# Every second chunk of expert weights asked for from ScalarE's queue

## The reference

```python
def hierarchical_moe(h, router_group, router_expert, w_gate, w_up, w_down):
    ...
    y = jnp.zeros_like(h)
    for e in range(N_EXPERTS):
        hid = jax.nn.silu(h @ w_gate[e]) * (h @ w_up[e])
        y = y + combine[..., e:e + 1] * (hid @ w_down[e])
    return y
```

## Time and profile before

| | |
|---|---|
| median of 3 runs | 3169.62 us (3167.96 to 3172.79) |
| profiled execution, its time | 3166.09 us |
| its span, from first to last instruction | 3164.3 us |
| granted TensorE clock, mean | 0.977 |
| PE busy | 2975.3 us (94%) |
| DVE, ACT busy | 1923.8 us, 1635.7 us |
| chunks asked for by SP in the whole kernel | 568, of which 192 in the expert stage |
| expert stage | the chunks are asked for from 843 to 1520 us of the span |

### The profile page before, as it was taken

One profiled execution on the slowest core, in us unless ns is written; L12 is line 12 of the kernel. 1 busy time (PEld: TensorE's weight loads), 2 busy tenths in 40 slices (PEclk: granted clock), 3 DMA queues, 4 the chain that ended last, 5 costly groups with the idle time before them and its releaser, 6 DMA issues.

```text
span 3164.3 us, 41302 instructions
## 1 busy us (share of the span) xinstructions
PE 2975.3 (94%) x16783; PEld 2592.6 (82%) x16783; DVE 1923.8 (61%) x2200; ACT 1635.7 (52%) x1942; POOL 175.2 (6%) x111
## 2 busy tenths in 40 slices
PE   4799999998979999999699999999989999999998
PEld 3798998897867777777599998888869999888886
DVE  3558644533468787888556675555545758555554
ACT  3354444433457777767555644444445554445443
POOL 0403100000000000000000100000000110000000
PEclk8899999999989999999899999999989999999999
DMA  4454557543649898989554555555545545555553
GB/s 150 142 165 147 204 189 243 201 149 120 201 154 352 286 345 284 336 291 360 180 167 160 173 187 186 173 176 183 180 138 190 172 149 194 179 185 173 174 186 133
DMA packets 322887, 629.31 MB, mean 199 GB/s; under 512 B 18425, under 2 KB 28178, under 8 KB 321298
## 3 DMA queue, kind: packets, MB, share of 16 engines
q1 hardware_dynamic: 319776, 617.03, 57.5%
q10 hardware_dynamic: 2642, 8.67, 0.7%
q0 software_dynamic: 288, 1.05, 0.1%
HBM read 619.36 MB, written 7.34 MB: 198 GB/s over the span
## 4 chain that ended last, share of the span: by engine, by line
PE 72%; DVE 10%; ACT 7%; issue 5%; DMA 5%; ACTq 0%; POOL 0%; DVEq 0%; SPq 0%; POOLq 0%
PE pairs L597 14%; PE pairs L599 14%; PE pairs L598 14%; PE pairs L607 8%; PE pairs L609 7%; PE pairs L611 7%; DVE w_lo L1739 5%; ACT w_hi L1240 2%; DMA raw<-in_w_gate_dram 2%; PE misc L985 2%; DMA raw<-in_w_up_dram 2%; PE misc L883 1%; PE misc L720 1%; PE misc L927 1%; ACT scratch L1574 1%
## 5 line engine op out<-in xcount | busy, mean ns | idle before, releaser
L1739 DVE TENSOR_TENSOR w_lo<-raw,w_hi 128x1024 fp32r<-128x1024 f32 x1136 | 1405.7, 1259 | 937.8 <-ACT w_hi L1240 930.8
L1240 ACT ACTIVATE w_hi<-raw 128x1024 fp32r<-128x1024 f32 x1136 | 1178.1, 1058 | 979.6 <-PE pairs L599 581.4
L597 PE MATMUL pairs<-w_hi,a_hi 128*128 128x512 f32 x1664 | 663.5, 399 | 27.5 <-DVE w_lo L1739 22.8
L599 PE MATMUL pairs<-w_hi,a_lo 128*128 128x512 f32 x1664 | 651.6, 392 | 0.0
L598 PE MATMUL pairs<-w_lo,a_hi 128*128 128x512 f32 x1664 | 651.6, 392 | 0.0
L607 PE MATMUL pairs<-a_hi,w_hi 128*128 128x256 f32 x1920 | 557.4, 290 | 47.6 <-DVE w_lo L1739 47.6
L609 PE MATMUL pairs<-a_lo,w_hi 128*128 128x256 f32 x1920 | 549.0, 286 | 0.0
L611 PE MATMUL pairs<-a_hi,w_lo 128*128 128x256 f32 x1920 | 548.5, 286 | 0.0
L607 PEld LDWEIGHTS pairs<-a_hi,w_hi 128*128 128x128 f32 x1920 | 373.8, 195 | 55.1 <-issue 31.4
L597 PEld LDWEIGHTS pairs<-w_hi,a_hi 128*128 128x128 f32 x1664 | 314.4, 189 | 111.8 <-DVE w_lo L1739 33.6
L609 PEld LDWEIGHTS pairs<-a_lo,w_hi 128*128 128x128 f32 x1920 | 374.3, 195 | 0.4
(11 more groups left out here) (312 smaller groups left out, 2315.5 us busy)
## 6 DMA issues: line engine op xcount, KB each, us to landing
raw<-in_w_in_dram SPq DMA_DIRECT2D x232, 1024.0 KB, 5.1
raw<-in_w_out_dram SPq DMA_DIRECT2D x80, 1024.0 KB, 5.0
raw<-in_w_gate_dram SPq DMA_DIRECT2D x64, 1024.0 KB, 7.2
raw<-in_w_up_dram SPq DMA_DIRECT2D x64, 1024.0 KB, 7.3
raw<-in_w_down_dram SPq DMA_DIRECT2D x64, 1024.0 KB, 6.1
raw<-in_xattn_wk_dram SPq DMA_DIRECT2D x16, 1024.0 KB, 5.0
raw<-in_xattn_wv_dram SPq DMA_DIRECT2D x16, 1024.0 KB, 5.0
raw<-in_xattn_wq_dram SPq DMA_DIRECT2D x16, 1024.0 KB, 5.1
```

Of the source, the lines that this page charges most:

```text
L597: nc.tensor.matmul(o, hi[:, k, tok], w_hi[:, s, q, :], start=k == 0, stop=False)
L599: m = nc.tensor.matmul(o, lo[:, k, tok], w_hi[:, s, q, :], start=False, stop=last)
L1240: a.activation(w_hi[:, i % HSLOTS], raw[:, i // 2, 2 * (i % 2):2 * (i % 2) + 2, :], ACT.Copy).then_inc(hi_done, 1)
L1739: v.tensor_tensor(w_lo[:, i % HSLOTS], raw[:, i // 2, 2 * (i % 2):2 * (i % 2) + 2, :], w_hi[:, i % HSLOTS].bitcast(F32), ALU.subtract).the ...
```

## The change

In the expert stage chunks 0 and 2 of every unit stay with SP. Chunks 1 and 3 are asked for by ACT, on its own queue, apart from those of the first unit. ACT has the request for chunk 1 of the next unit behind its half 5, and that for chunk 3 of the same unit behind its half 1. Each request waits for the same two counts as before. There are 47 x 2 = 94 such requests. The other stages are unchanged.

```diff
@@ SyncE @@
-            for g in range(GROUPS):
-                for i in range(PER_GROUP):
-                    e = PER_GROUP * g + i
-                    for r, ww in enumerate((w_gate, w_up)):
-                        for c in range(CHUNKS):
-                            chunk(c, moe_h(g, 2 * i + r) + 2 * c + 2, ww[:, e, 4 * c:4 * c + 4, :])
-                for n in range(4):
-                    for c in range(CHUNKS):
-                        chunk(c, moe_h(g, E0 + n) + 2 * c + 2,
-                              w_down[:, PER_GROUP * g + c, :, n * COLS:(n + 1) * COLS])
+            for n in range(GROUPS * UNITS_G):
+                for c in range(CHUNKS):
+                    if n == 0 or c % 2 == 0:
+                        chunk(c, H["moe"] + n * HALVES + 2 * c + 2, moe_chunk(n, c))
@@ ScalarE, in run() @@
                     state[0] += 1
+                    n = (h - H["moe"]) // HALVES
+                    if h % HALVES == 5 and 0 <= n < GROUPS * UNITS_G - 1:
+                        load(n + 1, 1)
+                    if h % HALVES == 1 and 0 < n < GROUPS * UNITS_G:
+                        load(n, 3)
+
+            def load(n, c):
+
+                count = H["moe"] + n * HALVES + 2 * c + 2
+                act.wait_ge(hi_done, count)
+                act.wait_ge(lo_done, count)
+                act.dma_start(raw[:, c], moe_chunk(n, c)).then_inc(landed[c], 16)
```

More of the change, by code:

```diff
@@ L459, in moe_h, with moe_chunk @@
             return H["moe"] + HALVES * (UNITS_G * g + i)
+        def moe_chunk(n, c):
+            g, i = n // UNITS_G, n % UNITS_G
+            if i < E0:
+                return (w_gate, w_up)[i % 2][:, PER_GROUP * g + i // 2, 4 * c:4 * c + 4, :]
+            return w_down[:, PER_GROUP * g + c, :, (i - E0) * COLS:(i - E0 + 1) * COLS]
         def gather_bank(g, c):
```

## The result

The changed kernel takes 3173.32 us (median; 3169.15 to 3178.63), the kernel before on the same chip 3166.30 us (3160.65 to 3172.79). The ratio is 1.0022, with the interval 1.0015 to 1.0029: the change costs 7.0 us. The profiled execution of the changed kernel took 3170.03 us, 3.9 us more than that of before, so the traces show only a good half of the loss, and single traces scatter by as much. The times decide here, the traces show where to look.

What follows compares the result with a forecast made beforehand. PE was taken as the bound, busy 2975.3 of 3164.3 us, with 23.9 us idle in the expert stage. The terms 0 + 0 + 5 + 0 = +5 us on the median 3169.62 gave 3174.6 us; whole range 3156 to 3197 us.

Steps and rivals of the forecast that it cites:

- What SP gives up: Expert stage: SP's 0.37 us issue is hidden within 3.00 us per chunk, so taking 94 requests off it frees 0 us.
- What ACT pays: Gate units after half 5: ACT's request makes `hidden_hi` 0.30 us late once per expert, 16 x 0.30 = 4.8, say 5 us.
- When ACT asks: Expert stage: ACT's requests come at the same time or at most about 1.4 us later, within the slack; cost 0.
- the slack of 2.6 us: Full stretch: a request may be about 2.6 us later before the DMA engines run dry.
- What two queues do to one another: Full stretch: older chunks land later, but engines stay full and landings stay 3.00 us apart; 0, bounds 0 and 21 us.
- the prediction's own signs of being right: Last gate and up units of a group: DMA share 1.00 with 350 GB/s, stretch within 47.98 + 4 x 0.5 us.
- rival A: Full stretch: shared engines delay the older chunk, 21 us on top of the 5, 3195.6 us; chance 0.30.
- A's two signs: Expert stage: landing times of SP's chunks above 7.8 us, and ACT's waits for landings above 63.5 us in total.
- Rival B: Full stretches: two queues keep the DMA engines better filled, above 360 GB/s, 12 us faster, 3157.6 us; chance 0.20.
- The doubt held against B: Full stretch: the engines' share is 1.00 already, start-of-kernel transfers have partly longer rows, and PE has little idle time.
- Rival C: Gate units: the 0.30 us falls into waits that are there anyhow, nothing reaches PE; 3169.6 us, chance 0.20.

Runs made afterwards that it cites:

- e7: Against the changed kernel: from the second unit on ACT asks for all four chunks on its one queue, 188 requests; 3167.64 us, ratio to before 1.0007.
- e2: Against the changed kernel: SP asks for all chunks; ACT keeps its 94 waits and issues, each moving only 8 numbers; 3168.67 us, ratio to before 1.0012.
- e4: Against the changed kernel: the 16 requests directly ahead of `hidden_hi` go back to SP, ACT keeps 78; 3172.39 us, ratio to before 1.0023.
- e8: Against the changed kernel: SP asks for all chunks, chunk 1 only once ACT signals behind half 6; 3171.01 us, ratio to before 1.0018.
- e1: Against the changed kernel: ACT asks for chunk 1 behind half 6 instead of half 5; 3188.92 us, ratio to before 1.0079.
- e11: Against the kernel before: SP asks for 512 KB halves, each when its half slot is free, and ACT waits per half; 3150.80 us, ratio 0.9956.
- e3: Against the changed kernel: GpSimd instead of ACT asks for chunks 1 and 3 on its own queue; 3182.10 us, ratio to before 1.0054.

## Why the prediction was right, and where it was not

The forecast was 3174.6 us, +5 us, which is less than the 6.3 us that the prediction took as the least a measurement can tell from no change; measured were +7.0 us. The sign and the size hold. That 3174.6 lies only 1.3 us from the measured 3173.32 is luck: the median it started from, of three executions, was 3.3 us above that of twenty, and the step was 2 us too small. The account behind the step holds in part.

- **What SP gives up: 0.** Nothing in the runs speaks against it: from the second unit on e7 takes all requests off SP and isn't faster. The Trainium skill, page "DMA: Bandwidth & Descriptors", section "Issuing engines are not separate DMA queues", was right that a second issuing engine brings no bandwidth here. That it costs some is what these runs add.
- **What ACT pays: 16 x 0.30 us.** The mechanism is in the trace as described: request to next instruction 0.42 us (0.41 forecast), DVE short of half 6, PE's `w_lo` later. The size was about 12 x 0.33 = 4 us, not 16 x 0.30: the first of the four units with `hidden_hi` in a group has 6.30 us with and without the request. One of the four is a down unit, where the prediction put the cost at 0; it goes from 5.67 to 6.00 us like the gate units. On one queue this is about what is lost (e7 2.2 us, e2 3.8 us). With two queues no gain is seen when it is taken away (e4, 1.0023 against 1.0022).
- **When ACT asks: 0.** ACT's requests start on the median 0.09 us after the slot is free, SP's 0.07, as forecast; between 940 and 1525 us the latest begins 0.48 us after it. But the slack of 2.6 us isn't free even on one queue: e8, with one chunk in four late by 0.90 us on average, costs 5.7 us. On two queues the same lateness costs 25 us (e1).
- **What two queues do to one another: 0.** This is the step that failed, "landings still come 3.00 us apart". Landings became irregular: 7.8 and 9.5 us on the median for the chunks of one matrix by queue, single chunks up to 10.3 us (10.7 in e4) where the longest took 9.3 us, single waits of 2.7 us (3.6 us in e4) where the longest was 2.3 us, the share down to 0.95 and 51.07 us in one stretch, where the prediction's own signs of being right were 1.00 and no more than 49.98 us. By the timed runs the second queue costs 7.3 us without the request ahead of `hidden_hi` (e4 against the kernel before) and 3 to 5 us on top of ACT's price (the change against e2 and e7). That is rival A's mechanism at a sixth to a third of its 21 us, which assumed half the slack lost once per expert. Of A's two signs one came in part: single chunks of SP's took 10.3 us, but SP's medians rose to no more than 7.8 us in the stretch, and ACT's waits for landings fell, to 52.3 us. e1 comes to A's price when chunk 1 is late by 0.90 us on average.
- **Rival B** was false for queues: no full stretch of the change is above 360 GB/s; 333 GB/s in the one shown, and in the shortest 16 chunks of 1024 KB in 46.87 us, 358 GB/s. The doubt held against B, that a share of 1.00 leaves no room, was false too: e11 reaches 368 GB/s on one queue.
- **Rival C**, nothing reaches PE, is excluded by the interval of the change, which begins at 1.0015.

So that the sum came out is luck in part: it had one term of 4 us sized well, and one set to 0 that costs as much or more, and the two don't simply add. How much of the 7.0 us belongs to each isn't settled beyond the ratios given: the pairs that would separate them differ by about as much as they are uncertain.

A small part lies behind the stage. There the granted clock is between its two levels (1.2 and 2.4 GHz) while PE has little to do. Windows of the 20 us that begin 41.1 to 41.4 us after the first chunk of the next stage was asked for, of the kernel before:

```profile
1561.00:1581.00 20.00, 14.17 (x100) 13.56 (x99) 12.33 (x20) 10.10 (x15) 0.00 (x0) 0.74 0.49 162
```

and of the changed kernel:

```profile
1564.50:1584.50 20.00, 14.17 (x89) 13.56 (x88) 12.14 (x19) 9.06 (x15) 0.00 (x0) 0.66 0.47 157
```

PE is busy for the same 14.17 us, with 89 matmuls recorded instead of 100: 0.66 of full speed granted instead of 0.74. By 20 x 0.08 that is about 1.6 us, an estimate. DVE's halves agree: those of the changed kernel run 3.3 us behind at the end of the stage and 4.8 us behind from 1585 us on; 0.8 us of it comes back later, between 2229 and 2421 us. It is one execution each, and whether it recurs wasn't tried.

## What to carry to other kernels

Where one queue keeps the DMA engines full and the order of the chunks matters, as here, keep all of them on it: a second queue gives up the order, and a late request cost several times more (1.0079 against 1.0018). An issue in the list of a computing engine costs its 0.3 to 0.4 us where the next instruction has no slack, here in 12 places of 94; count the places, not the requests. When an engine waits for landings under a full DMA share, look at what it waits for before looking at who asks: smaller transfers, which let work start on the first part, gave 0.995 where no choice of queue gave anything.

## What the runs showed of the hardware

- A DMA share of 1.00 isn't the highest rate: 350 GB/s with 1 MB transfers, 366 to 368 GB/s with 512 KB ones at 1.01, over the same rows of 2048 bytes. Why wasn't settled.
- Two queues are served side by side: in e1 two chunks asked for 0.31 us apart on two queues landed 0.5 us apart, after 8.8 and 9.0 us, where on one queue landings came 3.00 us apart. The Trainium skill, page "DMA: Bandwidth & Descriptors", section "Queues, rings and completion order", says that each DMA engine goes round robin between the queues it has work for, and the trace agrees.
- Issuing a 1 MB transfer takes ACT 0.37 to 0.39 us, an 8-number one 0.31 us on the median, so the price is nearly all fixed. GpSimd takes 0.75 us for a 1 MB one (e3).
